# Two macaron layers with dilated and neighbourhood attention: group mixing at unit 19 instead of 16, final scaling by column halves

## What is computed

```
x = x + 0.5 * swiglu(rms_norm(x, g1), w_up1, w_down1)       # 2816 hidden columns
x = x + mixer(rms_norm(x, g_mix))
x = x + 0.5 * swiglu(rms_norm(x, g2), w_up2, w_down2)
```

```
lse_g = max_g + log(den_g)                        # per head and row, for each group g
mix_w = softmax(stack(lse_g), axis=0)
ya    = sum over g of mix_w[g] * out_g            # 4 heads of 64 columns
out   = (sigmoid(gate_a) * (ya @ w_a) + sigmoid(gate_b) * (yb @ w_b)) @ w_out
```

## Time and profile before

| | us |
|---|---|
| median of 3 runs (1149.08 to 1150.02) | 1149.88 |
| the profiled execution, its own time | 1150.65 |
| its span, first to last instruction | 1148.8 |
| TensorE busy (99% of the span) | 1134.7 |
| VectorE busy (67%) | 766.4 |
| ScalarE busy (51%) | 583.8 |
| GpSimd busy (7%) | 76.6 |

### The profile page before, as it was taken

One profiled execution on the slowest core, in us unless ns is written; L12 is line 12 of the kernel. 1 busy time (PEld: TensorE's weight loads), 2 busy tenths in 40 slices (PEclk: granted clock), 3 DMA queues, 4 the chain that ended last, 5 costly groups with the idle time before them and its releaser, 6 DMA issues.

```text
span 1148.8 us, 17172 instructions
## 1 busy us (share of the span) xinstructions
PE 1134.7 (99%) x6707; PEld 955.3 (83%) x6707; DVE 766.4 (67%) x981; ACT 583.8 (51%) x781; POOL 76.6 (7%) x116
## 2 busy tenths in 40 slices
PE   8999999999999999999999999999999999999997
PEld 6888888888878888888888888888887888888886
DVE  5866667756666676666686666677566577666665
ACT  6444445555544654444474444465555545544442
POOL 3622100000110000000000000000003000000000
PEclk9999999999999999999999999999999999999999
DMA  9866654744544565556556555656446546655551
GB/s 288 276 208 229 205 191 147 256 150 145 191 161 145 183 220 183 184 190 207 171 165 216 183 183 185 201 189 199 152 143 198 202 131 201 202 196 184 184 182 37
DMA packets 148246, 214.34 MB, mean 187 GB/s; under 512 B 9344, under 2 KB 114016, under 8 KB 147936
## 3 DMA queue, kind: packets, MB, share of 16 engines
q1 hardware_dynamic: 142960, 205.28, 53.9%
q0 software_dynamic: 4560, 6.97, 2.1%
q10 hardware_dynamic: 672, 1.37, 0.4%
HBM read 210.75 MB, written 5.12 MB: 188 GB/s over the span
## 4 chain that ended last, share of the span: by engine, by line
PE 94%; DVE 2%; issue 1%; ACT 1%; DMA 1%; SPq 0%; POOLq 0%; POOL 0%; DVEq 0%; ACTq 0%
PE banks L1273 25%; PE banks L1207 16%; PE banks L1209 15%; PE banks L1208 15%; PE banks L1271 14%; PE banks L1270 3%; PE banks L1421 1%; PE banks L1384 1%; PE banks L1245 1%; PE banks L1407 1%; PE banks L1453 1%; DMA raw<-ffn_w_up_dram 1%; DVE w_lo L864 1%; ACT w_hi L629 1%; DVE probs L1047 0%
## 5 line engine op out<-in xcount | busy, mean ns | idle before, releaser
L864 DVE TENSOR_TENSOR w_lo<-raw,w_hi 128x2048 fp32r<-128x2048 f32 x190 | 438.8, 2310 | 192.7 <-ACT w_hi L629 192.4
L629 ACT ACTIVATE w_hi<-raw 128x2048 fp32r<-128x2048 f32 x190 | 363.6, 1915 | 212.2 <-PE banks L1209 210.1
L1273 PE MATMUL banks<-a_both,w_hi 128*128 128x512 f32 x1232 | 439.4, 396 | 0.0
L1271 PE MATMUL banks<-a_both,w_lo 128*128 128x256 f32 x1408 | 364.3, 279 | 0.7 <-DVE a_both L889 0.7
L1271 PEld LDWEIGHTS banks<-a_both,w_lo 128*128 128x128 f32 x1408 | 265.4, 189 | 15.7 <-issue 1.0
L1273 PEld LDWEIGHTS banks<-a_both,w_hi 128*128 128x128 f32 x1232 | 231.2, 188 | 47.3
L1207 PE MATMUL banks<-w_hi,a_both 128*128 128x512 f32 (+1 forms) x448 | 176.6, 394 | 0.0
L1209 PE MATMUL banks<-w_hi,a_both 128*128 128x512 f32 (+1 forms) x448 | 171.6, 383 | 0.0
L1208 PE MATMUL banks<-w_lo,a_both 128*128 128x512 f32 (+1 forms) x448 | 171.2, 382 | 0.0
L1207 PE MATMUL banks<-w_hi,hT_hi 128*128 128x512 f32 x320 | 125.0, 390 | 0.0
L1209 PE MATMUL banks<-w_hi,hT_lo 128*128 128x512 f32 x320 | 124.5, 389 | 0.0
(11 more groups left out here) (119 smaller groups left out, 927.4 us busy)
## 6 DMA issues: line engine op xcount, KB each, us to landing
raw<-ffn_w_up_dram SPq DMA_DIRECT2D x172, 512.0 KB, 4.2
raw<-w_in_dram SPq DMA_DIRECT2D x92, 512.0 KB, 4.5
raw<-ffn_w_down_dram SPq DMA_DIRECT2D x88, 512.0 KB, 4.0
raw<-w_out_dram SPq DMA_DIRECT2D x16, 512.0 KB, 4.3
raw<-w_branch_b_dram SPq DMA_DIRECT2D x8, 512.0 KB, 4.4
raw<-ffn_w_up_dram SPq DMA_DIRECT2D x8, 256.0 KB, 5.9
bias_rows<-bias_kinds POOLq DMA_DIRECT2D x32, 64.0 KB, 4.0
bias<-bias_rows SPq DMA_DIRECT2D x2, 1024.0 KB, 7.2
```

The lines of the kernel that those rows point to most:

```text
L629: act.activation(w_hi[slot][:, :], raw[slot][:, :], ACT.Copy).then_inc(hi_done, 1)
L864: dve.tensor_tensor(w_lo[slot][:, :], raw[slot][:, :], w_hi[slot][:, :].bitcast(F32), ALU.subtract).then_inc(lo_done, 1)
L1271: mm = pe.matmul(pair[:, b, 0:SEQ], w_lo[slot][:, at:at + P], a_hi[:, k, :], start=False, stop=False)
L1273: mm = pe.matmul(pair[:, b, :], w, both, start=False, stop=k == KT - 1)
```

## The change

The table entry `MIX_AT` goes from 16 to 19, which moves `mix_weights` on VectorE and its exponential on ScalarE in both layers; GpSimd follows by its semaphore. At the end, VectorE scales only the right column half of each row tile, and ScalarE the left one, after the squares of that tile. SP sends the right half of each tile when VectorE is done, ScalarE's queue the left half when ScalarE is done: each request now has 128 partitions with 2 KB each. There are four requests of 256 KB, as before. ScalarE now waits for the norm factor and for the gain product of the left half, scales, waits for its own result, issues its DMA, and only then takes the squares of the second row tile.

```diff
-MIX_AT = 16
+MIX_AT = 19
...
+        left_ready = sem("left_ready")
...
+        def out_part(t, n):
+            r = t * (P // RUN)
+            return residues(out)[r:r + P // RUN, :, n * NB:(n + 1) * NB]
...
             for t in range(TT):
                 sp.wait_ge(result_ready, t + 1)
-                r = t * P // RUN
-                sp.dma_start(residues(out)[r, :, :], stream_part(xg, r)).then_inc(out_written, 16)
-            sp.wait_ge(out_written, 16 * STRIDE)
+                sp.dma_start(out_part(t, 1), xg[:, t, NB:2 * NB]).then_inc(out_written, 16)
+            sp.wait_ge(out_written, 16 * 2 * TT)
...
-            for g in range(4):
-                sum_squares(LAST, g)
             for t in range(TT):
-                act.wait_ge(result_ready, t + 1)
-                r = t * P // RUN + 1
-                act.dma_start(residues(out)[r, :, :], stream_part(xg, r)).then_inc(out_written, 16)
-            act.wait_ge(out_written, 16 * STRIDE)
+                for n in range(2):
+                    sum_squares(LAST, 2 * t + n)
+                act.wait_ge(rstd_ready, LAST + t + 1)
+                act.wait_ge(xg_ready, 2 * t + 1)
+                act.activation(xg[:, t, 0:NB], xg[:, t, 0:NB], ACT.Copy, scale=rstd[:, t:t + 1]).then_inc(left_ready, 1)
+                act.wait_ge(left_ready, t + 1)
+                act.dma_start(out_part(t, 0), xg[:, t, 0:NB]).then_inc(out_written, 16)
+            act.wait_ge(out_written, 16 * 2 * TT)
...
-                    dve.tensor_scalar(xg[:, t, :], xg[:, t, :], rstd[:, t:t + 1], None, ALU.mult).then_inc(result_ready, 1)
+                    dve.tensor_scalar(xg[:, t, NB:2 * NB], xg[:, t, NB:2 * NB], rstd[:, t:t + 1], None,
+                                      ALU.mult).then_inc(result_ready, 1)
```

## The result

| | before | changed |
|---|---|---|
| median of 4 runs, us | 1149.82 (1149.08 to 1150.02) | 1161.47 (1160.86 to 1162.27) |
| profiled execution, its own time | 1150.65 | 1162.27 |
| its span | 1148.8 | 1160.4 |
| start of the last matmul | 1140.69 | 1137.12 |
| from there to the end of the span | 8.11 | 23.28 |

The ratio is 1.0100, with a 95% interval of 1.0086 to 1.0114. The changed kernel was forecast at 1146.3 and faster; it is slower, and 13 us above the top of the range, 1148.3. The last two lines split the difference of the spans: everything up to the last matmul became 3.57 us shorter, and what follows it became 15.17 us longer. Not all of the 3.57 need be the change: TensorE's wait for x at the start was 2.0 us in the profile before and 0.6 here, and in later profiles of kernels with the old mixing place the last matmul starts anywhere from 1139.19 to 1140.69.

The account below looks back on a forecast made before the run. TensorE, carrying 94% of the chain of waits, was taken to bound the kernel. Mixing 3.16 plus tail 0.4 gave 3.6 us off 1149.88, so 1146.3 us; range 1145.3 to 1148.3.

Parts of the forecast that it names:

- Part 1, the mixing: Mixing moved from unit 16 to unit 19, both layers: TensorE's pauses go, gaining 3.16 us at no cost.
- Both pauses: TensorE's excess of 0.46 us turning in unit 17 and 1.12 us at unit 18's values and scores, in each layer.
- the gap: VectorE's 2.79 us wait for TensorE before unit 20's products, claimed to cover the 1.83 us group-weight chain.
- the two twins: Same TensorE work with and without a pause, units 18 against 16 and 17 against 19: 1.58 us excess per layer.
- The subtraction of unit 22: VectorE's weight subtraction beside GpSimd's multiply at the new place: held back 0.9 us, with slack over 5 us.
- Rival (b): GpSimd late for the turning of y, TensorE standing 5.7 us: 7.8 us slower, 1157.7; chance 0.05.
- (a): Second copy still late, unit 18's 1.12 us pause stays: 1148.6 us; chance 0.09.
- (d): Next stall surfaces in the same units, such as unit 20's products, half a microsecond per layer: 1147.3 us; chance 0.09.
- Part 2, the scaling: Output tail, halves scaled by VectorE and ScalarE: last issue 0.4 us earlier, between 0.3 and 0.6.
- The first tile's 0.3 us: Row tile 0, VectorE scaling 512 columns instead of 1024: 0.3 us freed, bringing the chain to the second tile earlier.
- Part 2, the landing: Output after the last issue: landing kept at 3.7 us, bounds 2.9 and 4.0, 0.8 gained to 0.3 lost.
- rival (c): Tail does nothing or loses, ScalarE's half late or requests landing later together (4.0): 1146.7 to 1147.0 us; chance 0.10.

Follow-up runs that it names:

- the kernel with the shape alone: The kernel before with only the changed kernel's output request shape, VectorE still scaling the whole tile: 1165.49 us, ratio 1.0136.
- the interleaved groups of 2, 4 and 8: The kernel before with each output request's DRAM rows dealt out in turn as 2 x 32, 4 x 16, 8 x 8: 1166.86, 1157.75, 1152.24 us.

## Why the prediction was wrong, step by step

**Part 1, the mixing: right.** Both pauses went, and the gap, the weights and GpSimd's end came where the prediction put them (339.2 against 339.8 to 340.0, y at 342.15 against 342.7). 3.16 us were forecast; 3.0 (1.7 to 3.8) were measured, and the two twins of the changed trace give 2 x (0.45 + 1.12) = 3.14. The subtraction of unit 22 was held by the multiply as forecast: 334.50 + 2.28 = 336.78, and it ended at 333.72 + 2.92 = 336.64; the first addition was held by it in turn, 336.64 + 1.30 = 337.94 against 337.80. Rival (b), GpSimd late for y, did not happen, although the sign came out as its was: slower for another reason. Rivals (a) and (d) did not happen either.

**Part 2, the scaling: right in sign, mis-sized.** VectorE's half took 0.49 us (0.46 forecast), ScalarE's 0.72 (0.63 forecast, from a square; its own row is longer). The statement that ScalarE's issue "delays nothing that the end waits for" was wrong by a little: the issue took 1.26 us, not 0.52, the square at 1138.05 started 0.96 us after its input was ready (VectorE's update from 1136.34 to 1137.09), and VectorE waited 0.21 us for the sums (the bracket at 1139.42). Of 0.4 us the last issue kept 4.02 - 3.88 = 0.14. The first tile's 0.3 us came (the last update starts 0.61 us after the start of the last matmul, 0.87 before), half of it went again on the way to the norm factor, and the second tile's scaling and issue gained 0.02 and not 0.13.

**Part 2, the landing: this step failed, and with it the prediction.** It said: "Nothing in the trace is that, and the bounds are 2.9 (alone) and 4.0". The landing was taken for a matter of bytes and partitions, so the nearest rows seemed to bound it, and 3.7 us was kept for it. It measured 18.6, from the last issue at 1141.00 to the last packet's end at 1159.60. The time of a request went here by the number of DMA engines that carried it: 16 before, two after. The stretch view shows the two, the kernel with the shape alone shows that nothing else is needed, and the interleaved groups of 2, 4 and 8 show the number following the dimension. "Again two requests of 256 KB" was true and beside the point; rival (c) had the right place (requests that land later) and a bound of 4.0 us that came from a request of another shape.

The Trainium skill ("DMA: Bandwidth & Descriptors", section "Why a DMA increments its semaphore by 16 and not by 1") has the rule: a request is given the largest number of engines, up to 16, that divides the slowest dimension of both its sides. By it 64 gives 16, and 2 with 128 gives 2; the shares of 0.13, 0.25 and 0.50 agree. They vary the DRAM side alone; that the SBUF side counts as well, no run here shows. The prediction weighed another page of the Trainium skill ("SBUF — State Buffer"), on partitions and ports, by which the tail would have gained 0.6 us, and not this one. Its ranking of the shapes (128 partitions better than 64) isn't borne out or refuted here: the two-engine limit hides it.

## What to carry to other kernels

Before one request replaces several, write down both of its sides as dimensions and look at the outermost one: a view such as "2 blocks of 64 rows" was carried by two DMA engines here, at 256 KB a request; other sizes weren't run. A changed shape isn't bounded by rows of other shapes, so its range must reach to the time at a few engines' rate, 51 GB/s for two here. A chain of small operations paid here once it stood behind the last copy that TensorE waits for in a unit, in a gap that another engine's wait makes anyway, and its cost includes what the GpSimd work that it sets off does to VectorE.

## What the runs showed of the hardware that was not expected

- The number of engines that carry a request follows the outermost dimension of its DRAM side: 2, 4 and 8 gave shares of 0.13, 0.25 and 0.50. Two queues with such requests at once got the same engines: the share stayed 0.13, and two packets stayed under way, while from 1142 to 1157 both queues sent 11 to 13 packets each microsecond. Two engines moved 51 to 52 GB/s then, and about half of that in the output's first microseconds (24 GB/s from 1140 to 1145 with 2 interleaved groups).
- ScalarE's first issue of the output took 1.13 to 1.26 us in the six kernels whose requests have two row dimensions (2, 4 or 8 outermost), and 0.52 to 0.55 us where a request has one. It doesn't go by the number of engines: with 2 it took 1.13 to 1.26 and with 8 1.21. Nor by the shape alone: the second issue, of the same shape, took 0.56 to 0.65. Why is open.
- A copying activation with a scale for each partition, 128 x 512 from SBUF, took 0.72 us, a square with sum 0.63.
- A VectorE scaling of two numbers per partition was held until a GpSimd addition ended: 1.20 us against 0.17.
